# Weight sums of a seven-product block, made in an HBM scratch instead of on chip

## The reference

```python
proj = rmsnorm(x, norm_mix) @ w_in      # 1024 -> cb cc cu q k v g ga gb
y_conv = short_conv_mixer(cb, cc, cu, conv_w, w_conv_out)
y_ret = retention_mixer(q, k, v, g, positions, ret_norm, w_ret_out)   # rotary by positions, decay per head
x = x + (sigmoid(ga) * y_conv + sigmoid(gb) * y_ret) @ w_o
x = x + square(relu(rmsnorm(x, norm_mlp) @ w_up)) @ w_down            # 1024 -> 4096 -> 1024
```

## Time and profile before

| | |
|---|---|
| median of 3 runs | 2097.36 us |
| the profiled execution | 2097.74 us |
| its span | 2095.7 us |
| PE / DVE / ACT / POOL busy | 99% / 75% / 51% / 1% |
| granted TensorE clock, mean | 0.997 |
| DMA: bytes moved, mean rate | 227.95 MB, 109 GB/s |

### The profile page before, as it was taken

How to read it: one execution, slowest core, us unless ns; L and a number is a source line. 1 busy time by engine, 2 the same in 40 slices (tenths; PEclk the granted TensorE clock), 3 DMA queues, 4 the chain that set the end, 5 groups by cost and what they waited for, 6 DMA issues and landing times.

```text
span 2095.7 us, 30777 instructions
## 1 busy us (share of the span) xinstructions
PE 2074.5 (99%) x12372; PEld 1870.7 (89%) x12382; DVE 1563.7 (75%) x2113; ACT 1068.2 (51%) x1522; POOL 27.3 (1%) x36
## 2 busy tenths in 40 slices
PE   9998999999999999999999999999999999999998
PEld 8887878878888899988999998888899988999997
DVE  8887785769656778866878886656778866868884
ACT  5776574645434445524555654434445534555653
POOL 0000000000000000000000000000000000000000
PEclk9999999999999999999999999999999999999998
DMA  5323222212322234432344353322234432444352
GB/s 186 112 101 107 84 81 71 91 66 91 100 90 82 81 111 141 141 110 91 121 111 120 114 169 100 103 91 81 91 101 141 146 106 91 121 114 121 113 177 81
DMA packets 63869, 227.95 MB, mean 109 GB/s; under 512 B 7216, under 2 KB 7600, under 8 KB 63600
## 3 DMA queue, kind: packets, MB, share of 16 engines
q1 hardware_dynamic: 59040, 208.83, 29.9%
q0 software_dynamic: 4544, 17.04, 4.8%
q10 hardware_dynamic: 144, 0.12, 0.0%
HBM read 223.86 MB, written 2.10 MB: 108 GB/s over the span
## 4 chain that ended last, share of the span: by engine, by line
PE 83%; DVE 3%; ACT 1%; issue 1%; DVEq 0%; ACTq 0%
PE bank L849 15%; PE bank L851 15%; PE bank L850 15%; PE bank L894 9%; PE bank L898 9%; PE bank L896 9%; PE bank L844 2%; PE bank L846 2%; PE bank L845 2%; PE bank L1104 1%; PE bank L1096 1%; ACT arena L1683 0%; PE bank L1173 0%; PE bank L1174 0%; PE bank L1172 0%
## 5 line engine op out<-in xcount | busy, mean ns | idle before, releaser
L1902 DVE TENSOR_TENSOR w_lo<-w_raw,w_hi 128x1024 fp32r<-128x1024 f32 x477 | 571.4, 1213 | 372.4 <-ACT w_hi L1275 370.7
L1275 ACT ACTIVATE w_hi<-w_raw 128x1024 fp32r<-128x1024 f32 x477 | 491.3, 1048 | 512.5 <-PE bank L851 333.0
L849 PE MATMUL bank<-h_both,w_hi 128*128 128x512 f32 x956 | 365.1, 382 | 0.5 <-DVE h_both L2071 0.3
L850 PE MATMUL bank<-h_both,w_hi 128*128 128x512 f32 x956 | 362.3, 379 | 0.0
L851 PE MATMUL bank<-h_both,w_lo 128*128 128x512 f32 x956 | 362.3, 379 | 0.0
L849 PE MATMUL bank<-y_hi,w_hi 128*128 128x512 f32 x920 | 351.3, 382 | 6.3 <-DVE y_lo L1954 3.1
L850 PE MATMUL bank<-y_lo,w_hi 128*128 128x512 f32 x920 | 349.3, 380 | 0.0
L851 PE MATMUL bank<-y_hi,w_lo 128*128 128x512 f32 x920 | 349.2, 380 | 0.0
L849 PEld LDWEIGHTS bank<-h_both,w_hi 128*128 128x128 f32 x956 | 180.7, 189 | 28.1 <-issue 2.3
L849 PEld LDWEIGHTS bank<-y_hi,w_hi 128*128 128x128 f32 x920 | 174.3, 189 | 33.3 <-issue 8.1
L850 PEld LDWEIGHTS bank<-h_both,w_hi 128*128 128x128 f32 x956 | 180.7, 189 | 25.9 <-issue 1.0
(11 more groups left out here) (340 smaller groups left out, 3621.3 us busy)
## 6 DMA issues: line engine op xcount, KB each, us to landing
w_raw<-in_stream SPq DMA_DIRECT2D x389, 512.0 KB, 3.6
w_raw<-in_stream POOLq DMA_DIRECT2D x30, 512.0 KB, 5.4
x<-in_x_t SPq DMA_DIRECT2D x8, 256.0 KB, 6.5
out_t<-x SPq DMA_DIRECT2D x8, 256.0 KB, 2.1
arena<-in_consts POOLq DMA_DIRECT2D x1, 1024.0 KB, 5.2
w_raw<-in_stream SPq DMA_DIRECT2D x2, 256.0 KB, 4.2
arena<-in_positions POOLq DMA_DIRECT2D x1, 256.0 KB, 6.0
vec_t<-in_vecs ACTq DMA_DIRECT2D x1, 112.5 KB, 3.5
```

The costliest lines, as they stand in the source:

```text
L849: pe.matmul(out, w_hi[:, slot, w], streamed(a_h), start=first, stop=False)
L850: pe.matmul(out, w_hi[:, slot, w], streamed(a_l), start=False, stop=False)
L1275: A.activation(w_hi[:, slot, w], w_raw[:, chunks.raw_slot[raw], w], ACT.Copy).then_inc(hi_ready, 1)
L1902: V.tensor_tensor(w_lo[:, slot, w], src[:, w], w_hi[:, slot, w].bitcast(F32), ALU.subtract).then_inc(lo_ready, 1)
```

## The change

All four sums of every block are made in HBM. The weight quarters of the thirty blocks lie in an input of their own, parts [30, 4, 128, 1024], and an internal HBM tensor weight_sums of the same shape takes the sums. POOL waits for lo_ready to reach 8, and then issues copies and accumulating transfers from HBM to HBM, each for a group of three blocks (1.57 MB): per group four copies and four additions in six stages. Groups are pipelined, one stage per round, in 15 rounds; ahead of a round POOL waits until all transfers of the earlier rounds have landed (sums_in). An accumulating transfer can only add, so T1 and T2 come out as sums of other signs, and the order of the stored quarters changes (not shown); the signs are made good by scale=-1 in two of the keep copies, by subtractions in y_mix (one of them now a scalar_tensor_tensor) and by reversed operands in two of the activation sums.

Every block now has seven plain loads by SP, three from parts and four from weight_sums; for the latter SP also waits on sums_in. A slot is free after one remainder, as with ordinary chunks. The three DVE subtractions, POOL's accumulating load and their waits are gone. The loads of decay and positions move from POOL to ACT's queue, at the end of the step fox_gate of the second half, which stands ahead of trig. Core of the diff:

```diff
+RAW_PART = {B11: 1, B22: 2, B21: 3}
+SUM_PART = {T1: 0, T2: 1, T3: 2, T4: 3}
+SUM_GROUP = 3
...
+            for place in SEVEN:
+                load(("parts", self.blocks, RAW_PART[place]) if place in RAW_PART else ("sums", self.blocks, SUM_PART[place]))
+            self.blocks += 1
...
+def summing(blocks):
+    stages = ((("copy", 0, ("parts", 0)), ("copy", 2, ("parts", 0))), (("add", 0, ("parts", 1)), ("add", 2, ("parts", 2))),
+              (("copy", 1, ("sums", 0)),), (("add", 1, ("parts", 2)),), (("copy", 3, ("sums", 1)),), (("add", 3, ("parts", 3)),))
+    groups = [slice(a, min(a + SUM_GROUP, blocks)) for a in range(0, blocks, SUM_GROUP)]
+    rounds, done, count = [], {}, 0
+    for now in range(len(groups) + len(stages) - 1):
+        transfers = [(group, *transfer) for n, group in enumerate(groups) if 0 <= now - n < len(stages)
+                     for transfer in stages[now - n]]
+        rounds.append((count, transfers))
+        count += len(transfers)
+        if now >= len(stages) - 1:
+            last = groups[now - len(stages) + 1]
+            done.update({block: count for block in range(last.start, last.stop)})
+    return rounds, done
...
                 sp.wait_ge(lo_ready, chunks.raw_free[c])
-                sp.dma_start(w_raw[:, slot, :], stream[c, :, :]).then_inc(raw_loaded[slot], 16)
+                if kind == "sums":
+                    sp.wait_ge(sums_in, 16 * sums_done[at[0]])
+                row = stream[at[0], :, :] if kind == "stream" else {"parts": parts, "sums": sums}[kind][at[0], at[1], :, :]
+                sp.dma_start(w_raw[:, slot, :], row).then_inc(raw_loaded[slot], 16)
...
         def _(pool):
-                    pool.wait_ge(o_copied, HEADS // 2)
-                    pool.dma_start(decay, ...).then_inc(decay_in, 16)
-                    pool.dma_start(sin_t.bitcast(I32), positions.partition_broadcast(P)).then_inc(decay_in, 16)
-            for third_done, slot, c in chunks.fourth_sums:
-                pool.wait_ge(lo_ready, third_done)
-                pool.dma_start(w_raw[:, slot, :], stream[c, :, :], accum_op=ALU.add).then_inc(fourth_in, 16)
+            def rows(of, group, n):
+                return {"parts": parts, "sums": sums}[of][group, n, :, :].rearrange("g p w -> p g w")
+            pool.wait_ge(lo_ready, 2 * RING)
+            for before, transfers in sum_rounds:
+                wait(pool, sums_in, 16 * before)
+                for group, form, to, (of, n) in transfers:
+                    if form == "copy":
+                        pool.dma_start(rows("sums", group, to), rows(of, group, n)).then_inc(sums_in, 16)
+                    else:
+                        pool.dma_start(rows("sums", group, to), rows(of, group, n), accum_op=ALU.add).then_inc(sums_in, 16)
...
-                keep(last, sum_)
+                keep(last, sum_, -1.0)
...
-                keep(kept(T, step, 1), sum_)
+                keep(kept(T, step, 1), sum_, -1.0)
...
             def fox_gate(step):          # ACT
+                if half == 1:
+                    act.wait_ge(o_copied, HEADS // 2)
+                    act.dma_start(decay, ...).then_inc(decay_in, 16)
+                    act.dma_start(sin_t.bitcast(I32), positions.partition_broadcast(P)).then_inc(decay_in, 16)
...
             def remainder(n, slot):      # DVE
-                if place == T1:
-                    loaded(2)
-                    dve.wait_ge(combined, 3 * group + 1)
-                    V.tensor_tensor(raw[1], raw[2], raw[1], ALU.subtract).then_inc(combined, 1)
                 dve.wait_ge(hi_ready, T.value("chunk", n + 1))
                 V.tensor_tensor(w_lo[:, slot, w], ..., ALU.subtract).then_inc(lo_ready, 1)
-                if place == B11:
-                    loaded(1)
-                    dve.wait_ge(lo_ready, T.value("chunk", n + 1))
-                    V.tensor_tensor(raw[0], raw[1], raw[0], ALU.subtract).then_inc(combined, 1)
-                elif place == T1:
-                    dve.wait_ge(lo_ready, T.value("chunk", n + 1))
-                    V.tensor_tensor(raw[0], raw[0], raw[2], ALU.subtract).then_inc(combined, 1)
```

More of the change, by code:

```diff
@@ L335, in __init__, with load @@
     def __init__(self, items):
-        self.operand, self.groups, raw = [], 0, 0
+        self.operand, self.source = [], []
         self.raw_slot, self.raw_loads, self.raw_free = [], [], []
-        self.fourth_sums = []
+        self.blocks, self.n_stream = 0, 0
         free, loads = [0] * RING, [0] * RING
-        def load():
+        def load(source):
             slot = free.index(min(free))
@@ L353, in __init__ @@
                 for _ in range(chunks):
-                    self.operand.append((None, len(self.raw_slot), None))
-                    free[load()] = len(self.operand)
+                    load(("stream", self.n_stream))
+                    self.n_stream += 1
                 continue
[L357 to L365, removed]
+            for place in SEVEN:
+                load(("parts", self.blocks, RAW_PART[place]) if place in RAW_PART else ("sums", self.blocks, SUM_PART[place]))
+            self.blocks += 1
 COUNTED = ("turn", "chunk", "used", "a_hi", "a_lo", "act_out", "vec", "stats", "sumsq_read", "halves", "seeds", "sums", "mixes")
@@ L428, in build @@
         first_chunk += delta(item)["chunk"]
-    assert stream.shape[0] == chunks.n_raw
+    assert stream.shape[0] == chunks.n_stream and parts.shape[0] == chunks.blocks
+    sums = nc.dram_tensor("weight_sums", (chunks.blocks, len(SUM_PART), P, CW), F32, kind="Internal").ap()
+    sum_rounds, sums_done = summing(chunks.blocks)
     ctx = ExitStack()
@@ L658, in build @@
         vecs_in = sem("vecs_in")
-        fourth_in = sem("fourth_in")
+        sums_in = sem("sums_in")
         raw_half = sem("raw_half")
@@ L1240, in raw_of @@
         def raw_of(T, n):
[L1243 to L1248, removed]
+            return chunks.operand[T.fixed["chunk"] + n]
         def runs_ahead(step):
@@ L1266, in round_ahead, with round_raw @@
             def round_ahead(n, slot):
[L1267 to L1274, removed]
+                round_raw(raw_of(T, n), slot, slice(0, used_columns(T, n)))
+            def round_raw(raw, slot, w):
+                act.wait_ge(raw_loaded[chunks.raw_slot[raw]], 16 * chunks.raw_loads[raw])
                 A.activation(w_hi[:, slot, w], w_raw[:, chunks.raw_slot[raw], w], ACT.Copy).then_inc(hi_ready, 1)
@@ L1887, in remainder @@
             def remainder(n, slot):
[L1889 to L1893, removed]
-                if place == T1:
-                    loaded(2)
-                    dve.wait_ge(combined, 3 * group + 1)
-                    V.tensor_tensor(raw[1], raw[2], raw[1], ALU.subtract).then_inc(combined, 1)
-                w = slice(0, used_columns(T, n))
-                src = raw[{B21: 3, T3: 1, B22: 2}.get(place, 0)]
+                raw, w = w_raw[:, chunks.raw_slot[raw_of(T, n)], :], slice(0, used_columns(T, n))
                 dve.wait_ge(hi_ready, T.value("chunk", n + 1))
-                V.tensor_tensor(w_lo[:, slot, w], src[:, w], w_hi[:, slot, w].bitcast(F32),
+                V.tensor_tensor(w_lo[:, slot, w], raw[:, w], w_hi[:, slot, w].bitcast(F32),
                                 ALU.subtract).then_inc(lo_ready, 1)
-                if place == B11:
-                    loaded(1)
-                    dve.wait_ge(lo_ready, T.value("chunk", n + 1))
-                    V.tensor_tensor(raw[0], raw[1], raw[0], ALU.subtract).then_inc(combined, 1)
-                elif place == T1:
-                    dve.wait_ge(lo_ready, T.value("chunk", n + 1))
-                    V.tensor_tensor(raw[0], raw[0], raw[2], ALU.subtract).then_inc(combined, 1)
             def join(step):
@@ L2922, in order_of_weights @@
             at = {"v": CV, "g": CG, "gb": CGB, "cc": CC, "cu": CU, "cb": CB, "ga": CGA}[kind] + 512 * half
-            out.append(quarters(w_in[layer][:, at:at + 512]) if args.get("seven") else group(w_in[layer], [(at, 512)]))
+            if args.get("seven"):
+                by_parts.append(quarters(w_in[layer][:, at:at + 512]))
+                continue
+            out.append(group(w_in[layer], [(at, 512)]))
             if kind == "v":
```

63 lines of the change are left out of this document (32 added, 31 removed).

## The result

The changed kernel takes 2103.7 us, median of 7 runs (2099.95 to 2106.54); the kernel before, beside it on the same chip, 2096.64 (2096.36 to 2098.62). The ratio is 1.003, with a 95% interval of 1.0021 to 1.004: slower by 6.3 us by the ratio, 7.1 between the medians. The profiled execution took 2103.7 us around a span of 2101.9, 6.2 us over the 2095.7 of before.

A forecast was written before the change was run, and what follows sets the result against it. PE was taken to bound every seven-product stage, all after 744 us. Terms: 0 (DVE) + 0 (loads) + 0 (sums hidden) + 10 + 0.5 = +10.5 us, 2108 us; own range 2101 to 2120, 8 in 10: 2100 to 2190.

The forecast's parts named there:

- DVE's 110 us, 0: Removing 90 DVE subtractions, 110 us of work, nearly all after 744 us under a full PE: worth 0.
- at most 2: Rival of a faster kernel: the removed DVE work brings PE at most 2 us; chance 0.03.
- The sums are hidden: POOL's HBM sums, 533 us of transfers in 554 us of room, end some 20 us before the first block: 0.
- The low ends: Lower bounds for the HBM sums per 512 KB unit: a copy 1.32 us, an addition 2.8 us.
- Loads beside the sums in 40 to 744 us, 0: Plain weight loads sharing DMA engines with the sums stay hidden by ring slots and made chunks: 0, at worst 10 us.
- the first reading: DMA queues take turns row by row; beside additions trig's inputs would be late by 8.5 us.
- the second one: One queue's transfer goes ahead whole; with two such waits trig would be late by 20 us.
- rival (2): Whole transfers of the sums delay weight loads in 40 to 744 us: 10 to 30 us more, 2120; chance 0.07.
- The move, 10 + 0.5: Decay and positions issued later, by ACT, delay trig and PE by 10 us, plus 0.5 us of half clock.
- The 0.5 for the clock: Added time at half clock after PE's gap at trig, around the wait at 505 us: +0.5 us.
- Rival (1): The sums outlast 744 us and slow nine seven-product blocks, 12 us each, halved: +55 us, 2163; chance 0.36.

The follow-up runs named there:

- e4: The kernel before without its 90 DVE subtractions and the waits on them, results left wrong: 2096.33 us, ratio 0.9995.
- e2: The kernel before with only the loads of decay and positions moved to ACT's queue, no sums in HBM: 2098.42 us, ratio 1.0006.
- e5: The changed kernel with POOL's sums begun after 60 chunks instead of 8, so that they run into the first seven-product blocks: 2119.49 us, ratio 1.0101.
- e8: e1 with POOL's seventh round of sums held back until lo_ready 60, past the first softmax stretch: 2096.6 us, ratio 0.9995.
- e1: The changed kernel with decay and positions issued by SP ahead of load 80, about 460 us, instead of by ACT: 2098.0 us, ratio 1.0004.
- e7: The changed kernel with sum transfers for groups of five blocks instead of three: 2106.78 us, ratio 1.0043.
- e3: The changed kernel with positions issued ahead of decay on ACT's queue, with a semaphore of their own that trig awaits: 2100.17 us, ratio 1.0013.
- e6: The changed kernel with sum transfers for groups of two blocks instead of three: 2102.46 us, ratio 1.0024.

## Why the prediction came out as it did

2108.0 us, own range 2101 to 2120, against 2103.7. The order of things was right: an unhidden wait at trig, nothing from DVE, sums that are hidden. By its steps:

**DVE's 110 us, 0.** Right: PE idles 0.09 us in 744 to 2078, and e4 gives 1.1 us, within the "at most 2". How the small steps that make up the 1.1 come about, with so little idle time to win, stays open. Busy time of an engine under a full PE isn't idle time of PE.

**The sums are hidden.** Right. The last transfer is issued at 691.73 us; with a landing of 12.9 us they end near 705, where I had 723. The 240 units of 512 KB took 23.3% of 2101.9 = 490 us of all engines' time, where I had 494. In the first 14 us, 37 to 51, the sums were copies only. Their queue then:

```profile
q0 software_dynamic: 800, 3.15, 60.7%
```

0.607 x 14 = 8.5 us for six units: 1.42 us a copy unit (I had 1.32). The 120 units of additions have the rest: (490 - 120 x 1.42) / 120 = 2.66 us (I had 2.8). The low ends were right. The reason that I gave, that the addition has just one read more and HBM as target changes nothing, agrees with these figures, but no run tries it by itself. In bandwidth, the copy moved 3.15 MB in 8.5 us of all engines' time, 370 GB/s. The Trainium skill (DMA: Bandwidth & Descriptors, Latency and other measured facts) has 207 to 214 for copies between HBM tensors, measured with 16 KB rows on the queues of SP and ACT; these copies, of 4 KB rows on POOL's queue, were faster, and for them the measurement decides.

**Loads beside the sums in 40 to 744 us, 0.** Right. The landing went from 3.3 us to 8.3 in the median, just over the 8 us of lead that I had worked out; ACT's waits for w_raw in that stretch are 3.8 us in all, and none of it reached PE, behind the three made chunks. Queues in 100 to 112 us:

```profile
q0 software_dynamic: 429, 1.69, 70.5%
q1 hardware_dynamic: 428, 1.56, 34.9%
```

Both queues moved the same number of rows. Equal numbers would also come from equal turns of several rows, but the order of the rows' starts in the trace settles it: at 100 to 106 us, and in other stretches like it, the mix of the two queues repeats after 32 rows, 16 of each, one per engine. So it is row by row, as the first reading had it. This fells the second one, the whole transfer that goes ahead, and rival (2) with it. I had taken it from the 6.3 us of a single load beside decay; but that load has eight rows per engine and decay has eight, so that both readings add about the same 3.0 us, and the row never told them apart. The rule of the Trainium skill on this (same page, Queues, rings and completion order), a whole packet of typically 9 to 17 descriptors before an engine turns, isn't seen here with that length; it would fit only if a packet is one row in these transfers.

**The move, 10 + 0.5: the step that failed, in size.** Measured: 4.28 us of waiting at trig, and 3.57 + 0.97 = 4.54 at PE, 0.35 of which it had before (4.5 in PE's stream). Its two parts were both too dear. Quiet, I had 2.9 us, out of a landing of 6.7; that landing was taken beside another load. Alone the inputs land in 5.0, and e2 has 0.83. For the traffic I had 5.6 by rows and more by whole transfers: it was 3.45. The queues beside trig show why:

```profile
q10 hardware_dynamic: 71, 0.58, 68.7%
q0 software_dynamic: 71, 0.24, 30.4%
```

```profile
q10 hardware_dynamic: 165, 0.61, 93.8%
q1 hardware_dynamic: 5, 0.02, 7.2%
q0 software_dynamic: 3, 0.01, 3.4%
```

The first is 478 to 480 us: ACT's queue (q10) and the sums' (q0). That they have 71 rows each is chance: up to 478 the sums have the engines to themselves, and from 479 they are running out (7 and 3 rows in half a microsecond, against 24 and 25 of ACT's). The sums' rows are copies here, 0.30 x 2 x 16 / 71 = 0.14 us each, not additions of 0.35. In 480 to 482 us the sums' queue is nearly dry. POOL had been held for 48.30 us at the last issue of its round and issued it only at 482.63. So the inputs had the engines almost alone for all but their first part. That is luck: nothing in the code puts this hold at trig. In e5 they met busy queues throughout, and the wait was 9.53: row-wise 8.5 was a fair figure for that case. The 0.5 for the clock didn't appear either. Windows after, behind PE's gap of 3.57 us:

```profile
502.00:504.00 2.00, 2.00 (x11) 1.76 (x10) 2.00 (x4) 2.00 (x4) 0.00 (x0) 1.00 1.03 418
```

The granted clock stayed at 1.00, 2.4 GHz. It had fallen to 0.5 behind the gap of 3.06 us at 198, before and after, and it stood at 0.50 in e5's row of 506 to 508 us above, behind a gap of 8.73 us. In e8 the same PE work at 201 to 204 us ran at 1.00, and the clock was down at 174 to 176 us instead:

```profile
174.00:176.00 2.00, 2.00 (x6) 1.55 (x6) 2.00 (x2) 0.00 (x0) 0.00 (x0) 0.50 1.02 418
```

One gap's clock wasn't to be carried over to another of like length. Had trig's wait been longer, the term would have been too small: behind e5's gap PE worked for 5 us at half clock, some 2.5 us.

**Not foreseen: +1.3 us** by POOL's issuing beside DVE's scaling (e8), which offsets the 1.1 us of e4. The last stores' 1.0 is chance, and the 0.5 of the clock at the end comes and goes between profiles. Together these are 1.3 - 1.1 + 0.5 + 1.0 = 1.7 us for which the prediction had no term; they brought the time nearer to 2108.0 than trig's wait alone would have.

**Rival (1), given 0.36.** Its condition was right in kind (554 us of room, 533 forecast, some 20 us to spare) and didn't come about. Its price of 12 us a block was wrong: e5 has 2.1. It used 1.32 + 2.8 to 4.1 us a load, 4.8 on average. With the measured units a load that lets in as many rows of the sums costs 1.32 + 1.42 = 2.7 beside copies, 4.0 beside additions, 3.4 on average, against 2.56 us of PE, 5.9 us a block; that the loads' lead and the gaps between rounds take up the rest, down to 2.1, is argued and not shown. Even e5, whose last transfer is issued 269 us past 744, took 2119.5, inside the range's lower third. The upper end of 2190 was paid for a term that was never that large.

## What to carry to other kernels

A load that is moved to another engine's queue is priced by when that engine reaches the place, and by what the queues hold then. If a serial chain behind it has no slack, every microsecond of its landing is one of the kernel; issue it early, from an engine that is at that place in time, as e1 did, and the cost is gone. Heavy background traffic on the DMA engines is free while the loads it slows have a lead longer than their stretched landing (here 8.3 us beside a ring of four slots and three made chunks), and it starts to cost where the loads' own rate nears the rate of use. Work taken off an engine that isn't the bound gives next to nothing: 110 us gave 1.1.

## What the runs showed of the hardware

- **GpSimd's issuing slows VectorE.** While POOL issued transfers of 1.57 MB, 0.76 us for one, DVE's scaling of 512 columns took up to 917 ns in place of 483; with the issues moved away (e8, e7) it was 482, with the transfers running. The Trainium skill (SBUF — State Buffer, Who interferes with whom) says that the two share one pair of ports as an exclusive lock; the rows agree in that DVE's operation is held while POOL issues, and it cost PE 1.3 us in two places; why it is this pair of engines no run takes apart.
- **GpSimd's issue is held at set counts of what it has issued.** POOL's eighth issue of the round at 427 us waited 48.30 us, with nothing in the profile for it to wait on but the issue itself. Seven transfers outstanding aren't the reason: the round at 306 us puts out eight in a row, and the one at 237 us is held at its fifth.

```profile
273.32 2.51 POOL L777 DMA_DIRECT2D weight_sums<-in_parts  x2 [32.50 <-issue]
309.20 3.41 POOL L777 DMA_DIRECT2D weight_sums<-in_parts  x2
310.73 3.39 POOL L775 DMA_DIRECT2D weight_sums<-in_parts  x2
```

The holds come after 28 and 55 issues of 384 rows, and at the same two counts in e1, e3, e5 and e8, whatever the time. In e6 they come after 42 and 82 issues of 256 rows (and once more, after 60), in e7 after 18 and 34 of 640: in rows 10752, 10752 and 11520 for the first, 21120, 20992 and 21760 for the other. What is full then no run shows. Whatever stands behind the issue on POOL waits too.

- **HBM to HBM:** 1.42 us of all 16 engines for 512 KB copied, 2.66 added; the second is near the accumulating load into SBUF, 2.8.
- **Two queues share the engines row by row,** so that a transfer's landing stretches with the rows of the other queue, and in the median not with the size of its transfers (8.1, 8.3 and 8.5 us for groups of two, three and five).
